# Attention of the sample group: score and value matmuls cut into four column groups of 32

## The chip, the cores and the metric

The kernel runs on one core of a Trainium2 chip. The metric is the device time of one execution in microseconds (us), as the median of several executions.

## The reference

One inference step of a two-layer decoder trunk over two groups of tokens with shared weights: a prompt of 1024 tokens and 8 samples of 4 new tokens each (32 tokens, `NS`). Width is 1024, 16 heads of 64. Layer 0 mixes by a gated short convolution, layer 1 by stick-breaking attention; each layer then has a ConvFFN of hidden width 2816. A final norm ends it. Everything is float32.

The stage in question is the attention of the samples. Each sample has 256 past tokens in two pages of 128 and its own 4 new tokens. With `z = q.k / 8 + bias_h`, over the keys s before the query t:

```
log_keep = where(mask, log_sigmoid(-z), 0)
after    = cumsum(log_keep, reverse) - log_keep
w        = where(mask, exp(log_sigmoid(z) + after), 0)
o        = einsum('bhqk,bkhd->bqhd', w, v)
```

The keys and values of the past are read through a page table that is known only at run time.

## The kernel before, in words

Each engine has a program of its own, written out in order; semaphores tie them. Weights are streamed tile by tile by SP (SyncE) as `raw`, split by GpSimd into a high and a low half (`w_hi`, `w_lo`), and TensorE does three fp32r matmuls per tile and block (lines 442, 445, 446). That is how all projections and FFNs run. The prompt attention follows the QKV projection (lines 555 to 615); after it comes the sample attention, and then the output projection `wo` and the second FFN.

The sample attention works on pairs of samples, `bp` = 0 to 3. A pair fills 128 rows: row 64*b + 4*head + t for sample b of the pair. `q_rows` holds the queries with zeros, so that chunk c of the features (heads 2c and 2c+1) has nonzero columns only at the rows of these two heads. Each chunk's matmul thus adds to the rows of its heads, and eight chunks make all heads.

- `sample_scores(bp)` (line 669) on TensorE: for each of 8 chunks and each of 2 samples one matmul with 64 columns of weights and 256 keys as the moving side (line 678); the two samples write partitions 0 to 63 and 64 to 127. Then 8 matmuls with all 128 columns against the 32 new keys (line 683), and one that adds the mask (line 685).
- ScalarE takes two sigmoids of the scores (`beta_s`, `keep_s`; line 997 onwards). VectorE scans and multiplies (`sample_weigh`, lines 1326 and 1328).
- `sample_turn(bp)` (line 688): three transposes of the weights by TensorE; VectorE copies them to `w_ts` (`sample_copy`, lines 1332 and 1333).
- `sample_values(bp)` (line 696): w times v. Two matmuls with 32 rows and 128 columns against the new values (`v_new`, line 704), then 8 matmuls with 64 columns against the V pages (line 712), each 512 wide: all heads of a half of the features. The result is 128 x 1024, over two PSUM banks. All rows get all 16 heads' features, and only the diagonal blocks (a row's own head) are used.
- `sample_rows(bp)` (line 1003) on ScalarE copies these 128 x 1024 to `o_rows`; `sample_out(bp)` (line 717) turns them in 8 transposes (line 722) into both banks of `spare`; `sample_take(bp)` (line 1335) on VectorE picks the diagonal blocks in 16 copies of 64x8 (line 1344) into `mixed`.

TensorE's order is: scores of pair 0; then for each pair `bp`: scores of bp+1, `sample_out` of bp-1, turn of bp, values of bp; at the end `sample_out` of the last pair. ScalarE has one code line for all its activations (line 744).

The pages come on SP's queue. Four page buffers of K and four of V hold two pairs. Pages of pairs 0 and 1 are loaded long before. For pairs 2 and 3 SP goes in this order: four K loads of 512 KB for pair 2 (line 393), after scores of pair 0; four V loads for pair 2 (line 399), after values of pair 0; the page numbers for pair 3, read with register loads (line 385); four K loads for pair 3, after scores of pair 1; four V loads for pair 3, after values of pair 1. SP's wait for a pair's values thus also stands ahead of the next pair's K loads. At the same time ScalarE's queue brings back x (8 times 528 KB), which was spilled to memory.

An fp32 matmul is two instructions with the same line in the trace, each with a load of weights of its own (LDWEIGHTS, engine PEld); a transpose is one.

Of the kernel before, what the change touches and what calls it, by code (L numbers as in the profile page):

```python
# [21 lines left out]
P = 128  # L22
D = 1024
KC = D // P
SEQ = 1024
NB, NT = 8, 4
NS = NB * NT
# [7 lines left out]
PAGES, PG = 2, 128  # L35
PAST = PAGES * PG
# [109 lines left out]
def build(nc, x_in, weights, taps_sc, taps_ffn, state_sc, state_ffn, gains, bias_heads, bias_rows,  # L146
# [6 lines left out]
    with ctx:  # L153
# [7 lines left out]
        def at(offset, name, shape, dt):  # L161
            return nc.alloc_sbuf_tensor_at(name, shape, dt, offset=offset)

        def size(shape, dt):
            n = 1
            for d in shape[1:]:
                n *= d
            return -(-n * (2 if dt == bf16 else 4) // 32) * 32

        def sb(name, shape, dt=f32):  # L170
            t = at(top[0], name, shape, dt)
            top[0] += size(shape, dt)
            assert top[0] <= base + arena, name
            return t
# [10 lines left out]
        ident = sb("ident", [P, P])  # L185
# [18 lines left out]
        mixed = sb("mixed", [P, KC, T])  # L204
# [15 lines left out]
        k_s = sb("k_s", [P, KC, NS])  # L220
# [16 lines left out]
        page_k = [sb(f"page_k{n}", [P, KC, PAGES, PG]) for n in range(4)]  # L237
        page_v = [sb(f"page_v{n}", [P, PAGES, D]) for n in range(4)]
# [2 lines left out]

        q_rows = [sb(f"q_rows{n}", [P, KC * (P + 2 * NT)]) for n in range(2)]
        v_new = sb("v_new", [NS, D])
        o_rows = sb("o_rows", [P, D])
        beta_s = [sb(f"beta_s{n}", [P, PAST + NS]) for n in range(2)]
        keep_s = [sb(f"keep_s{n}", [P, PAST + NS]) for n in range(2)]
        prod_s = sb("prod_s", [P, PAST + NS])
        w_ts = sb("w_ts", [P, PAGES + 1, P])
# [4 lines left out]
        out = [bank[0], bank[1]]  # L253
        spare = bank[2]
# [4 lines left out]
        score = [out[1][:, 0:2, :].rearrange("p a b -> p (a b)"), spare[:, :, :].rearrange("p a b -> p (a b)")]  # L259
# [2 lines left out]

        turned = [out[0][:, 2, :], out[1][:, 2, :]]
        attended = out[0][:, 1, :]
        o_s = out[0][:, 0:2, :].rearrange("p a b -> p (a b)")

        def sem(name):
            return ctx.enter_context(nc.semaphore(name))
# [12 lines left out]
        s_o_rows = sem("s_o_rows")  # L281
        s_o_turned = sem("s_o_turned")
# [56 lines left out]
        s_out = sem("s_out")  # L339
# [99 lines left out]
        def _(pe):  # L439
# [225 lines left out]
            for c in range(KC):  # L665
                mm = nc.tensor.transpose(score[1][0:NS, c * P:(c + 1) * P], v_s[:, c, :], ident[:, :])
            mm.then_inc(s_vturned, 1)

            def sample_scores(bp):

                pe.wait_ge(s_set, bp + 1)
                bank_s = out[1][:, bp % 2, :]
                for b in range(2):
                    pe.wait_ge(page_k_in[2 * (bp % 2) + b], (bp // 2 + 1) * 32)
                for c in range(KC):
                    for b in range(2):
                        slot, rows = 2 * (bp % 2) + b, slice(64 * b, 64 * b + 64)
                        nc.tensor.matmul(bank_s[rows, 0:PAST], q_rows[bp % 2][:, c * P + 64 * b:c * P + 64 * b + 64],  # L678
                                         page_k[slot][:, c, :, :].rearrange("p g t -> p (g t)"),
                                         start=c == 0, stop=c == KC - 1, skip_group_check=True)  # L680

                for c in range(KC):
                    nc.tensor.matmul(bank_s[:, PAST:PAST + NS], q_rows[bp % 2][:, c * P:(c + 1) * P], k_s[:, c, :],
                                     start=c == 0, stop=False, skip_group_check=True)
                nc.tensor.matmul(bank_s[:, PAST:PAST + NS], ident_b[:, :], new_b[:, bp, :], start=False,
                                 stop=True, skip_group_check=True).then_inc(s_scored, 1)

# [8 lines left out]
            def sample_values(bp):  # L696

                pe.wait_ge(s_wt, bp + 1)

                if bp:  # L700
                    pe.wait_ge(s_o_rows, bp)

                for half in range(2):
                    nc.tensor.matmul(out[0][:, half, :], w_ts[0:NS, PAGES, :], v_new[:, 512 * half:512 * half + 512],
                                     start=True, stop=False, skip_group_check=True)
                for b in range(2):
                    pe.wait_ge(page_v_in[2 * (bp % 2) + b], (bp // 2 + 1) * 32)
                for half in range(2):
                    for g in range(PAGES):
                        for b in range(2):  # L710
                            slot, rows = 2 * (bp % 2) + b, slice(64 * b, 64 * b + 64)
                            mm = nc.tensor.matmul(out[0][rows, half, :], w_ts[:, g, rows],
                                                  page_v[slot][:, g, 512 * half:512 * half + 512], start=False,
                                                  stop=g == PAGES - 1, skip_group_check=True)
                mm.then_inc(s_full, 1)

            def sample_out(bp):
                pe.wait_ge(s_o_rows, bp + 1)

                pe.wait_ge(s_out, bp + 1)  # L720
                for c in range(KC):
                    mm = nc.tensor.transpose(score[1][:, c * P:(c + 1) * P], o_rows[:, c * P:(c + 1) * P], ident[:, :])
                mm.then_inc(s_o_turned, 1)

            sample_scores(0)
            pe.wait_ge(s_vnew, 1)
            for bp in range(NB // 2):
                if bp + 1 < NB // 2:
                    sample_scores(bp + 1)
                if bp:  # L730
                    sample_out(bp - 1)
                sample_turn(bp)
                sample_values(bp)
            sample_out(NB // 2 - 1)
            pe.wait_ge(s_out, NB // 2 + 1)
            tiles_of("wo", T_WO, H_WO)
# [5 lines left out]
        def _(act):  # L742
            def act_op(o, i, func=ACT.Copy, **kw):
                return nc.scalar.activation(o, i, func, **kw)  # L744
# [257 lines left out]

            def sample_rows(bp):
                act.wait_ge(s_full, bp + 3)
                act_op(o_rows[:, :], o_s).then_inc(s_o_rows, 1)

            sample_sigmoids(0)
            for bp in range(NB // 2):
                if bp + 1 < NB // 2:
                    sample_sigmoids(bp + 1)  # L1010
                sample_rows(bp)
# [19 lines left out]
        def _(dve):  # L1031
            V = nc.vector
# [302 lines left out]
            def sample_take(bp):  # L1335

                dve.wait_ge(s_o_turned, bp + 1)
                for h in range(2):
                    rows = slice(DH * h, DH * h + DH)
                    o = mixed[rows, :, SEQ + bp * 2 * NT:SEQ + (bp + 1) * 2 * NT].rearrange("p c (b t) -> p c b t", b=2)  # L1340

                    r = score[1][rows, :].rearrange("p (c b r) -> p c b r", c=KC, b=2)
                    for c in range(KC):
                        last = V.tensor_copy(o[:, c, :, :], r[:, c, :, 8 * c + 4 * h:8 * c + 4 * h + NT])
                last.then_inc(s_out, 1)

            sample_q(0)
# [4 lines left out]
            for bp in range(NB // 2):  # L1352
                sample_copy(bp)
                if bp + 2 < NB // 2:
                    sample_q(bp + 2)
                if bp + 1 < NB // 2:
                    sample_weigh(bp + 1)
                if bp:
                    sample_take(bp - 1)
            sample_take(NB // 2 - 1)  # L1360

            for n in range(2):
# [113 lines left out]
```

## Time and profile before

| | us |
|---|---|
| median of 3 runs | 2736.73 (2732.05 to 2737.2) |
| profiled execution, its own time | 2740.34 |
| its span, first to last instruction | 2738.3 |
| TensorE matmuls busy | 2612.5 (95%) |
| VectorE busy | 1450.5 (53%) |
| ScalarE busy | 508.7 (19%) |
| GpSimd busy | 715.5 (26%) |
| DMA | 149.00 MB, mean 54 GB/s |

Busy time of TensorE counts modelled ends of matmuls that overlap, so a stream of matmuls is better read by its starts. "PEclk" is the granted clock of TensorE: 1.00 is 2.4 GHz and 0.50 is 1.2 GHz. A DMA share of 1.0 means that all 16 engines of the core are busy. In the rows PE is TensorE's matmuls, PEld its weight loads, DVE VectorE, ACT ScalarE, POOL GpSimd and SPq the queue of SP.

### The profile page before, as it was taken

To read this page: it belongs to the slowest core of one execution; us is meant where nothing else is said; L and a number is where in the kernel's file an instruction comes from. 1 tells how busy PE (TensorE), PEld (TensorE's weight loads), DVE (VectorE), ACT (ScalarE), POOL (GpSimd) and SP (SyncE) were. 2 spreads that over 40 slices of the span, in tenths; PEclk is the share of its full clock that TensorE was granted. 3 is DMA by queue.
4 is the path that set the end of the run, shared out by engine and by line. 5 is a ranking of instruction groups with operands and counts; after the bars stand their busy time and mean duration, and the time that the engine had idled before them with its cause. 6 is when DMAs were issued, how large, how long until landed. Compare 5 with 4: busy or idle time off the path is not lost.

```text
span 2738.3 us, 40374 instructions
## 1 busy us (share of the span) xinstructions
PE 2612.5 (95%) x16774; PEld 2474.4 (90%) x16774; DVE 1450.5 (53%) x1328; ACT 508.7 (19%) x905; POOL 715.5 (26%) x405
## 2 busy tenths in 40 slices
PE   6999999999999999988999999789999999999995
PEld 6999999999999999977888888559899999999995
DVE  6333436444444444466777777633654444444446
ACT  3000112000000000124444444420200000000012
POOL 3333323322233332321111111002323222333332
PEclk9999999999999999999999999999999999999997
DMA  3111111111111111131111111631111111111111
GB/s 128 47 47 47 41 46 46 41 46 47 47 47 47 40 46 39 50 110 39 40 40 40 40 47 40 206 120 47 39 39 47 47 47 47 47 47 47 47 42 63
DMA packets 58213, 149.00 MB, mean 54 GB/s; under 512 B 5458, under 2 KB 25682, under 8 KB 58066
## 3 DMA queue, kind: packets, MB, share of 16 engines
q1 hardware_dynamic: 49186, 122.42, 13.8%
q10 hardware_dynamic: 8880, 24.29, 2.3%
q8 instruction: 132, 2.16, 0.3%
q14 instruction: 15, 0.12, 0.0%
HBM read 128.91 MB, written 17.78 MB: 54 GB/s over the span
## 4 chain that ended last, share of the span: by engine, by line
PE 88%; DVE 7%; issue 2%; ACT 2%; DMA 1%; SPq 0%; DVEq 0%; ACTq 0%
PE bank L442 26%; PE bank L446 26%; PE bank L445 25%; PE bank L615 3%; PE bank L555 3%; PE bank L588 2%; DVE h_lo L1062 1%; DVE x L1160 1%; DVE y L1150 1%; ACT a_hi L744 1%; DVE total L1072 1%; DVE h_lo L1108 1%; PE bank L453 1%; PE bank L558 0%; PE bank L678 0%
## 5 line engine op out<-in xcount | busy, mean ns | idle before, releaser
L442 PE MATMUL bank<-h_hi,w_hi 128*128 128x352 f32 x3648 | 1195.5, 328 | 40.2 <-DVE h_lo L1062 21.7
L446 PE MATMUL bank<-h_hi,w_lo 128*128 128x352 f32 x3648 | 1179.4, 323 | 0.0
L445 PE MATMUL bank<-h_lo,w_hi 128*128 128x352 f32 x3648 | 1175.5, 322 | 0.0
L442 PEld LDWEIGHTS bank<-h_hi,w_hi 128*128 128x128 f32 x3648 | 688.1, 189 | 56.6 <-issue 36.6
L416 POOL CAST w_hi<-raw 128x1024 fp32r<-128x1024 f32 x196 | 212.5, 1084 | 1960.9 <-PE bank L442 1914.1
L445 PEld LDWEIGHTS bank<-h_lo,w_hi 128*128 128x128 f32 x3648 | 692.7, 190 | 0.0
L446 PEld LDWEIGHTS bank<-h_hi,w_lo 128*128 128x128 f32 x3648 | 688.7, 189 | 0.0
L418 POOL TENSOR_TENSOR w_lo<-raw,w_hi 128x1024 fp32r<-128x1024 f32 x196 | 493.2, 2517 | 15.7
L1160 DVE TENSOR_TENSOR x<-x,bank 128x1056 f32<-128x1056 f32 x192 | 238.8, 1251 | 319.1 <-PE bank L446 319.1
L442 PE MATMUL bank<-a_hi,w_hi 128*128 128x352 f32 x1056 | 343.4, 325 | 8.5 <-DVE x L1160 8.5
L445 PE MATMUL bank<-a_lo,w_hi 128*128 128x352 f32 x1056 | 341.5, 323 | 0.0
L446 PE MATMUL bank<-a_hi,w_lo 128*128 128x352 f32 x1056 | 340.8, 323 | 0.0
L1139 DVE TENSOR_TENSOR ext<-bank,rstd 128x1056 f32<-128x1056 f32 x44 | 55.4, 1259 | 344.2 <-PE bank L446 344.1
L442 PEld LDWEIGHTS bank<-a_hi,w_hi 128*128 128x128 f32 x1056 | 198.3, 188 | 16.8 <-DVE x L1160 16.3
L1263 DVE TENSOR_TENSOR_SCAN prod<-keep 128x895 f32<-128x895 f32 (+7 forms) x128 | 195.0, 1524 | 15.6 <-ACT keep L744 11.3
L445 PEld LDWEIGHTS bank<-a_lo,w_hi 128*128 128x128 f32 x1056 | 198.3, 188 | 0.0
L446 PEld LDWEIGHTS bank<-a_hi,w_lo 128*128 128x128 f32 x1056 | 198.3, 188 | 0.0
L744 ACT ACTIVATE smp<-ext 128x32 f32<-128x32 f32 x52 | 12.0, 231 | 965.4 <-DVE ext L1139 878.7
L744 ACT ACTIVATE beta<-bank,bias_pair 128x896 f32<-128x896 f32 (+7 forms) x128 | 95.0, 742 | 221.3 <-PE bank L558 217.3
L1152 DVE TENSOR_TENSOR a_lo<-y,a_hi 128x1056 fp32r<-128x1056 f32 x44 | 106.8, 2428 | 52.4 <-ACT a_hi L744 52.4
L1267 DVE TENSOR_TENSOR beta<-beta,prod 128x895 f32<-128x895 f32 (+7 forms) x128 | 127.2, 994 | 4.4
L1114 DVE TENSOR_SCALAR y<-ext,tap_ffn 128x1024 f32<-128x1024 f32 x44 | 115.8, 2631 | 9.7 <-DVE ext L1139 9.6
(104 smaller groups left out, 1654.3 us busy)
## 6 DMA issues: line engine op xcount, KB each, us to landing
raw<-weights SPq DMA_DIRECT2D x196, 512.0 KB, 3.4
page_k<-cache_k SPq DMA_DIRECT2D x16, 512.0 KB, 7.0
page_v<-cache_v SPq DMA_DIRECT2D x16, 512.0 KB, 6.3
x_spill<-x ACTq DMA_DIRECT2D x8, 528.0 KB, 6.4
k_out<-k_t ACTq DMA_DIRECT2D x8, 528.0 KB, 2.7
v_out<-v_t ACTq DMA_DIRECT2D x8, 528.0 KB, 2.7
x<-x_spill ACTq DMA_DIRECT2D x8, 528.0 KB, 7.4
y_out<-y_rows ACTq DMA_DIRECT2D x3, 1408.0 KB, 5.2
```

What stands on the lines that cost most here:

```text
L416: nc.gpsimd.tensor_copy(w_hi[ring][:, :], raw[slot][:, :]).then_inc(w_high, 1)
L418: nc.gpsimd.tensor_tensor(w_lo[ring][:, :], raw[slot][:, :], w_hi[ring][:, :].bitcast(f32), ALU.subtract).then_inc(w_split, 1)
L442: mm = nc.tensor.matmul(o, w_hi[w][:, c0:c0 + P], hi, start=first, stop=False)
L445: nc.tensor.matmul(o, w_hi[w][:, c0:c0 + P], lo, start=False, stop=False)
L446: return nc.tensor.matmul(o, w_lo[w][:, c0:c0 + P], hi, start=False, stop=last)
L555: nc.tensor.matmul(score[h][:, n0:n1], q_t[par][rows, i * P:(i + 1) * P], k_t[par][rows, n0:n1], start=True, stop=n1 < width)
L744: return nc.scalar.activation(o, i, func, **kw)
L1114: V.tensor_scalar(o[:, 0:SEQ], e[:, 0:SEQ], tap(0), None, ALU.mult).then_inc(tapped, 1)
L1152: V.tensor_tensor(a_lo[:, slot, par, :], y[par][:, :], a_hi[:, slot, par, :].bitcast(f32), ALU.subtract).then_inc(a_ready, 1)
L1160: V.tensor_tensor(xx, xx, result(s), ALU.add).then_inc(taken[s], 1)
L1263: V.tensor_tensor_scan(prod[:, width - 1:0:-1], back, back, 1.0, ALU.mult, ALU.bypass).then_inc(scanned, 1)
L1267: V.tensor_tensor(w[:, 0:width - 1], w[:, 0:width - 1], prod[:, 1:width], ALU.mult).then_inc(weighed, 1)
```

## The change

Row 64*b + 32*g + ... holds heads 0 to 7 of sample b for g = 0 and heads 8 to 15 for g = 1. The change gives each of these four groups of 32 rows matmuls of its own, with 32 columns of weights. Chunks 0 to 3 concern only the groups g = 0 and chunks 4 to 7 only g = 1, so the number of score matmuls on pages stays at 16 for a pair, in the order b, g inside each of four rounds. The 8 matmuls against the new keys become 16. The values of a group need only the 512 features of its 8 heads: the result is 128 x 512 in one bank, the two matmuls on `v_new` with 128 columns become 4 with 32, and the 8 on V pages with 64 columns become 8 with 32. The bank alternates with the pair. The row copy is 128 x 512 into one of two `o_rows`, the transposes are 4 into one of two banks of `spare`, and the take is 8 copies of 64x16. Waits are for the use two pairs ago where they were for the last one.

```diff
-        o_rows = sb("o_rows", [P, D])
+        o_rows = [sb(f"o_rows{n}", [P, D // 2]) for n in range(2)]
...
-        o_s = out[0][:, 0:2, :].rearrange("p a b -> p (a b)")
+        o_s = [out[0][:, n, :] for n in range(2)]
+        o_turned = [spare[:, n, :] for n in range(2)]
...
-                for c in range(KC):
+                for cc in range(KC // 2):
                     for b in range(2):
-                        slot, rows = 2 * (bp % 2) + b, slice(64 * b, 64 * b + 64)
-                        nc.tensor.matmul(bank_s[rows, 0:PAST], q_rows[bp % 2][:, c * P + 64 * b:c * P + 64 * b + 64],
-                                         page_k[slot][:, c, :, :].rearrange("p g t -> p (g t)"),
-                                         start=c == 0, stop=c == KC - 1, skip_group_check=True)
-
-                for c in range(KC):
-                    nc.tensor.matmul(bank_s[:, PAST:PAST + NS], q_rows[bp % 2][:, c * P:(c + 1) * P], k_s[:, c, :],
-                                     start=c == 0, stop=False, skip_group_check=True)
+                        for g in range(2):
+                            c, r = cc + g * KC // 2, 64 * b + 32 * g
+                            nc.tensor.matmul(bank_s[r:r + 32, 0:PAST], q_rows[bp % 2][:, c * P + r:c * P + r + 32],
+                                             page_k[2 * (bp % 2) + b][:, c, :, :].rearrange("p g t -> p (g t)"),
+                                             start=cc == 0, stop=cc == KC // 2 - 1, skip_group_check=True)
+
+                for cc in range(KC // 2):
+                    for b in range(2):
+                        for g in range(2):
+                            c, r = cc + g * KC // 2, 64 * b + 32 * g
+                            nc.tensor.matmul(bank_s[r:r + 32, PAST:PAST + NS], q_rows[bp % 2][:, c * P + r:c * P + r + 32],
+                                             k_s[:, c, :], start=cc == 0, stop=False, skip_group_check=True)
...
-                if bp:
-                    pe.wait_ge(s_o_rows, bp)
-
-                for half in range(2):
-                    nc.tensor.matmul(out[0][:, half, :], w_ts[0:NS, PAGES, :], v_new[:, 512 * half:512 * half + 512],
-                                     start=True, stop=False, skip_group_check=True)
+                if bp >= 2:
+                    pe.wait_ge(s_o_rows, bp - 1)
+
+                for r in range(0, P, 32):
+                    g = r // 32 % 2
+                    nc.tensor.matmul(o_s[bp % 2][r:r + 32, :], w_ts[0:NS, PAGES, r:r + 32],
+                                     v_new[:, 512 * g:512 * g + 512], start=True, stop=False, skip_group_check=True)
                 for b in range(2):
                     pe.wait_ge(page_v_in[2 * (bp % 2) + b], (bp // 2 + 1) * 32)
-                for half in range(2):
-                    for g in range(PAGES):
-                        for b in range(2):
-                            slot, rows = 2 * (bp % 2) + b, slice(64 * b, 64 * b + 64)
-                            mm = nc.tensor.matmul(out[0][rows, half, :], w_ts[:, g, rows],
-                                                  page_v[slot][:, g, 512 * half:512 * half + 512], start=False,
-                                                  stop=g == PAGES - 1, skip_group_check=True)
+                for page in range(PAGES):
+                    for r in range(0, P, 32):
+                        b, g = r // 64, r // 32 % 2
+                        mm = nc.tensor.matmul(o_s[bp % 2][r:r + 32, :], w_ts[:, page, r:r + 32],
+                                              page_v[2 * (bp % 2) + b][:, page, 512 * g:512 * g + 512], start=False,
+                                              stop=page == PAGES - 1, skip_group_check=True)
...
-                pe.wait_ge(s_out, bp + 1)
-                for c in range(KC):
-                    mm = nc.tensor.transpose(score[1][:, c * P:(c + 1) * P], o_rows[:, c * P:(c + 1) * P], ident[:, :])
+                pe.wait_ge(s_out, max(bp, 1))
+                for cc in range(KC // 2):
+                    mm = nc.tensor.transpose(o_turned[bp % 2][:, cc * P:(cc + 1) * P],
+                                             o_rows[bp % 2][:, cc * P:(cc + 1) * P], ident[:, :])
...
-                act_op(o_rows[:, :], o_s).then_inc(s_o_rows, 1)
+                if bp >= 2:
+                    act.wait_ge(s_o_turned, bp - 1)
+                act_op(o_rows[bp % 2][:, :], o_s[bp % 2]).then_inc(s_o_rows, 1)
...
-                    r = score[1][rows, :].rearrange("p (c b r) -> p c b r", c=KC, b=2)
-                    for c in range(KC):
-                        last = V.tensor_copy(o[:, c, :, :], r[:, c, :, 8 * c + 4 * h:8 * c + 4 * h + NT])
+                    r = o_turned[bp % 2][rows, :].rearrange("p (c b g r) -> p c b g r", c=KC // 2, b=2, g=2)
+                    for c in range(KC // 2):
+                        last = V.tensor_copy(o[:, c, :, :, :], r[:, c, :, :, 8 * c + 4 * h:8 * c + 4 * h + NT])
```

## Rows read from the trace of the kernel before

**Rows 1.** The page, part 1: busy us, share of the span, instructions.
```profile
PE 2612.5 (95%) x16774; PEld 2474.4 (90%) x16774; DVE 1450.5 (53%) x1328; ACT 508.7 (19%) x905; POOL 715.5 (26%) x405
```

**Rows 2.** Windows, stage: start:end, us, busy by engine, PEclk, DMA share, GB/s.
```profile
1767.95:1829.90 61.95, 52.80 (x320) 29.14 (x320) 14.74 (x87) 7.69 (x13) 0.00 (x0) 0.95 0.59 196
```

**Rows 3.** Windows of 2 us, for the granted clock (third number from the end).
```profile
1770.00:1772.00 2.00, 2.00 (x16) 1.18 (x14) 0.00 (x0) 0.00 (x0) 0.00 (x0) 0.77 0.99 395
1812.00:1814.00 2.00, 2.00 (x7) 0.60 (x8) 0.58 (x8) 0.00 (x0) 0.00 (x0) 0.50 0.00 0
1834.00:1836.00 2.00, 2.00 (x9) 2.00 (x9) 2.00 (x2) 2.00 (x3) 1.92 (x2) 0.56 0.00 0
```

**Rows 4.** Chain of waits through the stage: start us, us, what.
```profile
1767.95 5.12 PE bank L678 x32
...
1787.19 0.35 SPq L399
...
1791.83 0.56 SPq L393
...
1795.62 6.85 DMA page_k<-cache_k
...
1802.61 3.67 PE bank L678 x32
...
1812.24 5.14 PE bank L712 x16
...
1829.10 0.76 DVE mixed L1344 x8
```

**Rows 5.** Who waited for whom, 1760 to 1835: total us, times, longest.
```profile
PE bank L678 <- DMA page_k<-cache_k: 2.6, 1, 2.6
```

**Rows 6.** Timeline of TensorE streams: start us, us, engine, line, tiles, count.
```profile
1782.12 0.18 PEld L704 LDWEIGHTS bank<-v_new,w_ts 32*128 32x128 f32 x1 [0.24 <-issue]
1782.55 0.18 PEld L704 LDWEIGHTS bank<-v_new,w_ts 32*128 32x128 f32 x1 [0.24 <-issue]
1784.41 0.14 PEld L712 LDWEIGHTS bank<-page_v,w_ts 128*64 128x64 f32 x2 [0.29 <-issue]
1784.84 0.14 PEld L712 LDWEIGHTS bank<-page_v,w_ts 128*64 128x64 f32 x2 [0.28 <-issue]
1783.50 3.65 PE L712 MATMUL bank<-page_v,w_ts 128*64 128x512 f32 x16
1774.92 3.67 PE L678 MATMUL bank<-page_k,q_rows 128*64 128x256 f32 x32
1773.00 1.97 PE L683 MATMUL bank<-k_s,q_rows 128*128 128x32 f32 x16
1759.01 0.88 PE L615 MATMUL bank<-w_first,v_rows 128*64 128x128 f32 x12 [1.70 <-ACT w_first L744]
1827.29 1.09 PE L722 MATMUL bank<-ident,o_rows 128*128 128x128 f32 x8 [1.12 <-ACT o_rows L744]
```

**Rows 7.** Timeline of ScalarE and VectorE: row copies, weights of pair 0, the take.
```profile
1826.21 1.02 ACT L744 ACTIVATE o_rows<-bank 128x1024 f32<-128x1024 f32 x1 [7.79 <-PE bank L712]
1776.81 0.46 DVE L1328 TENSOR_TENSOR beta_s<-beta_s,prod_s 128x287 f32<-128x287 f32 x1
1765.11 0.60 ACT L744 ACTIVATE mixed<-bank 128x512 f32<-128x512 f32 x1 [0.79 <-PE bank L615]
1828.42 1.43 DVE L1344 COPY mixed<-bank 64x8 f32<-64x8 f32 x16 [6.53 <-PE bank L722]
1767.51 0.39 DVE L1316 COPY q_rows<-q_s 64x64 f32<-64x64 f32 x2
```

**Rows 8.** Windows of 0.5 us, for the DMA engines (last two numbers).
```profile
1784.50:1785.00 0.50, 0.50 (x6) 0.20 (x4) 0.00 (x0) 0.00 (x0) 0.00 (x0) 1.00 0.24 71
1786.00:1786.50 0.50, 0.50 (x4) 0.14 (x2) 0.00 (x0) 0.00 (x0) 0.00 (x0) 1.00 0.00 0
1788.50:1789.00 0.50, 0.50 (x8) 0.35 (x6) 0.00 (x0) 0.00 (x0) 0.00 (x0) 1.00 0.65 229
```

More of the change, by code:

```diff
@@ L1339, in sample_take @@
                     rows = slice(DH * h, DH * h + DH)
-                    o = mixed[rows, :, SEQ + bp * 2 * NT:SEQ + (bp + 1) * 2 * NT].rearrange("p c (b t) -> p c b t", b=2)
-                    r = score[1][rows, :].rearrange("p (c b r) -> p c b r", c=KC, b=2)
-                    for c in range(KC):
-                        last = V.tensor_copy(o[:, c, :, :], r[:, c, :, 8 * c + 4 * h:8 * c + 4 * h + NT])
+                    o = mixed[rows, :, SEQ + bp * 2 * NT:SEQ + (bp + 1) * 2 * NT].rearrange("p (g c) (b t) -> p c b g t", g=2, b=2)
+                    r = o_turned[bp % 2][rows, :].rearrange("p (c b g r) -> p c b g r", c=KC // 2, b=2, g=2)
+                    for c in range(KC // 2):
+                        last = V.tensor_copy(o[:, c, :, :, :], r[:, c, :, :, 8 * c + 4 * h:8 * c + 4 * h + NT])
                 last.then_inc(s_out, 1)
```

## The prediction

> **What bounds the kernel now.** I read the page first [rows 1]: TensorE is busy for 95% of the span, so time taken off its stream is time off the end, unless a transfer is late there. The diff touches one stage only. The chain of waits puts it between the first score matmul at 1767.95 us and the last copy of the sample outputs, which ends at 1829.88 [rows 4]: 61.95 us, 2.3% of the span, with TensorE busy for 52.80 us and the DMA engines at 0.59 [rows 2]. That is all the change can touch.
>
> Read in order, the chain [rows 4] says what ends last inside it. Up to 1787.2 it is TensorE. Then it leaves TensorE: the end of the first values lets SP issue the V pages of pair 2 (1787.19), behind them SP reads page numbers and issues the K pages of pair 3 (1791.83), and the chain waits for these until 1802.6. TensorE had done its work by 1800.1 and stood 2.6 us for them [rows 5]. From 1802.61 to 1829.88 (27.3 us) nothing is loaded that anybody waits for, and the path is TensorE with one ScalarE copy and one set of VectorE copies per pair. So the stage has three parts: TensorE, page transfers, TensorE again.
>
> **Does four in turn overlap as two do?** Each fp32 matmul is two instructions in the trace. With all 128 columns of weights the 512-wide one starts every 0.43 us, one at a time (1782.12, 1782.55); with 64 columns two start together every 0.43 us [rows 6]. So two column groups overlap completely: 16 instructions are 8 steps of 0.43 (3.65 us with the tail of the last), and the 32 score instructions at 256 wide are 16 steps of 0.216 (3.67 us) [rows 6]. The number of instructions stays: 32 for scores, 16 for page values. Only if four groups overlap are there 8 and 4 steps. Nothing in this trace has four groups at once; the bounds are a step of four at the price of a step of two (all saved) and at the price of four single ones (each step twice as long for the same count). I take the first, because the second member of a pair adds nothing that can be seen (0.43 against 0.43), and the groups write different partitions.
>
> The Trainium skill (TensorE: Matmul & The Clock Gate, section Measured speedup vs the span model) gives 2.38 for three column tiles with 512 columns, not 3. By that a step of four would be a quarter longer, 0.27 and 0.54 by estimate, and the tail below would lose 1.8 us of its gain. This trace has full overlap at two and none of three.
>
> **Working, from 1802.6 to the end** (warm clock):
> - Scores of pair 3: 8 steps of 0.216 fewer: -1.73.
> - Scores against the new keys: now 16 instructions, 0.112 apart, 1.97 us [rows 6]. They become 32 with a quarter of the weights and 32 columns. Bounds: 0.22 us, if four groups overlap and time scales with columns from 0.216 for 256; and 1.74, if an instruction can't be fed faster than the fastest stream here, 12 in five steps of 0.11 plus the tail (0.88 us), 0.054 each [rows 6]. I take 0.9, between them: -0.9 (ends 0 and -1.6).
> - v_new: 4 single steps of 0.43 become 8 instructions in 2 steps, in values of pairs 2 and 3: 2 x -0.86 = -1.72.
> - Page values: 8 steps become 4: 2 x -1.72 = -3.44.
> - Transposes of the outputs: 8 become 4, at 0.109 each (1.09 us for 8 [rows 6]); three calls lie on the path: 3 x -0.44 = -1.31.
> - ScalarE's copy of the rows: 128x1024 took 1.02, and a 128x512 out of PSUM 0.60 [rows 7]: 2 x -0.42 = -0.84. It is exposed for pairs 2 and 3 and hidden behind scores for 0 and 1.
> - The last take: 16 copies of 64x8 in 1.43 us, 0.09 each; 8 copies of 64x16 at about 0.1 (64x64 costs 0.2) [rows 7]: -0.65. The takes before it lie beside page values.
> - The transpose, copy and wait from the weights to v_new (1.2 to 1.3 us, twice) stay.
>
> Sum -10.6. The new waits (the row copy on the turning of two pairs ago, the turning on the take of two pairs ago) are looser than those replaced, and nothing queues behind them.
>
> The Trainium skill (TensorEngine Tiling, section Instruction Overhead) speaks against splitting the new-key matmuls: some 60 cycles each, so a short free dimension should not be tiled. By that estimate 32 take 0.8 us and not 0.2, and the sum stays within 0.1 of the above. No row here has such short ones in column groups.
>
> **The clock.** TensorE's granted clock was 0.5 (1.2 GHz) when the stage began and full from about 1771 (0.77 in that window); it fell to 0.5 again at 1812 [rows 3], and the page values of pair 2 took 5.14 [rows 4] instead of 3.65 [rows 6]: +1.5 in the time before. After the change TensorE stands longer for pages (about 5 us twice, below), and its work between the waits of the tail is half as long. The bounds: no low stretch (-1.5), or low for the whole tail, whose TensorE streams then sum to 9.8 us (scores 1.73 and 0.9, turnings of outputs 3 x 0.44, of weights 2 x 0.35, v_new 2 x 0.86, pages 2 x 1.72), so +9.8 - 1.5. The next stage too began at 0.5, until shortly before 1836 (0.56 in the window before [rows 3]), some 3.3 us of matmuls, which costs 1.7. I take one such stretch and a little, 2.2 in place of 1.5: +0.7. Tail: -9.9.
>
> **Before 1802.6.** Score streams of pairs 0 and 1 save 1.9 (partly cold) and 1.75, the new keys about 0.9 each, the values of pair 0 0.86 + 1.72: they end 8 us earlier, at about 1779. The chain from the scores of pair 0 to its weights ends at 1777.27 with VectorE's multiplication (1776.81 and 0.46 [rows 7]), 2.3 us after these scores, and so still fits beside the scores of pair 1. But the pages don't come 8 us earlier. From 1766.5 to 1784 the DMA engines are full (0.99 in the first window of rows 3) with x coming back (8 times 528 KB) and the K pages of pair 2; the last bytes of these land at about 1786, and the engines idle only until the V pages start at about 1788.4 [rows 8]. Order in the one queue stays: K2, V2, K3. V2 is now issued before K2 is in, so V2 starts between 1784.5 (engines thinning to 0.24) and 1786: 2.4 to 3.9 us earlier. K3 follows as before, since its issues are ready in time (4.6 us after V2's). I take -3.3. So of 8 us some 5 turn into TensorE standing for K2 and then for K3. The other transfers: V3 is issued after K3 and lands 5 to 7 us after it, before values of pair 3 need it; weights for the next stage are already split three tiles ahead.
>
> Sum -3.3 - 9.9 = **-13.2 us**. The profiled execution took 2740.34 for its span of 2738.3; the runs' median 2736.73 is 3.6 lower, a fixed offset that I keep: 2736.73 - 13.2 = **2723.5 us**.
>
> **Rivals.**
> - A, four overlap, as above: 2723.5. Its own range: saving 7.6 (K3 2.4 earlier, new keys nothing, clock +4.5, half way to D) to 17 (3.9, new keys -1.6, no low clock): 2720 to 2729. Chance 0.74.
> - B, the change doesn't do what it says: only two at a time are in flight, for example because the two halves of one matmul share a group and a step takes the late half of one and the early half of the next. For it: the pairs in rows 6 can be read so. Against it: the first step has two already, and the count of steps is exactly half that of instructions. Scores, v_new and page values stay; the new keys -0.9, transposes -1.3, copies -0.84 and -0.65 in the tail, and V2 issued about 1.8 us earlier by two new-key streams: -4.2 (2.8 to 5.5), 2732.5. Chance 0.12.
> - C, slower: 32-column matmuls run one after another, in the score and value streams. Scores +3.46, page values +3.44, v_new +1.72 per pair. On the path before K3 stand two score streams and one of values (+12), in the tail one and two (+13.8), less 2.8: +23, 2760. For it: four moving streams from memory at once are nowhere in the trace. Against: two don't disturb each other. Between B and C the cost is linear: it turns slower once more than about 0.15 of the overlap of pairs is lost. Chance 0.05.
> - D, four overlap but the clock is low for the whole tail: -10.6 + 8.3 - 3.3 = -5.6, 2731. For it: the drop at 1812 came with TensorE partly idle. Against: 5 us of busy time at 1766 raised it. Chance 0.07. 0.02 is left for others.
>
> A measurement of this kernel can tell about 0.2% (5.5 us) from no change. A and half of D are faster, B and the rest the same, C slower: 0.79, 0.15, 0.06. The range takes A from below and B and D from above: 2718 to 2733.5.
>
> **What would show it.** Four 32-column instructions starting within some 20 ns, every 0.216 us in scores and 0.43 in values; scores of 1.9 us and page values of 1.9. Two waits of TensorE for page_k, of 4 to 7 us each, where there was one of 2.6. DMA engines without a hole at 1786 to 1788. Less than 18 us from the scores of pair 3 to the last take. I am wrong if starts come in twos (B) or singly (C), if K3 lands as long after the stage's start as before, or if the granted clock is 0.5 for more than 5 us after K3.

## The result, and the profile after

Five executions of the changed kernel: median 2715.28 us (2712.78 to 2722.12), against 2736.59 (2732.05 to 2737.2) for five of the kernel before; ratio 0.9932, 95% interval 0.9918 to 0.9946. That is 21.3 us less, below the forecast's range. Twelve more executions, taken with the experiments, gave medians of 2720.54 and 2719.87 for six each. All 17 together have a median of 2719.87 and a mean of 2719.2; all 95 executions of the kernel before 2736.57 and 2736.4. So the change is worth 17.2 us (15.3 to 19.1, from the means), 0.6% of the kernel. A part of the first 21.3 was the luck of five executions: their median lies 4.7 us below that of the next twelve (2720.0).

The chain of waits of the changed kernel through the stage (start us, us, what); compare [rows 4]:

```profile
1759.50 3.33 PE bank L680 x32
...
1765.09 4.42 SPq L394
1769.70 2.47 SPq L394
1772.27 1.61 SPq L400
...
1778.18 0.56 SPq L394
...
1782.98 6.84 DMA page_k<-cache_k
...
1789.95 3.46 PE bank L680 x32
...
1796.40 1.90 PE bank L717 x16
...
1805.40 0.46 DVE mixed L1352 x4
```

The stage begins at 1759.50 and ends at 1805.86: 46.4 us instead of 61.9. TensorE leaves the chain after the first scores; from 1763 to 1790 the chain is SP's issuing and the page transfers. K of pair 3 is there 30.5 us after the start, not 34.7; from there to the end it is 15.9 us, not 27.3.

The timeline of the changed kernel, for [rows 6] and [rows 7] (start us, us, engine, line, tiles, count):

```profile
1768.29 0.13 PEld L717 LDWEIGHTS bank<-page_v,w_ts 128*32 128x32 f32 x4 [0.30 <-issue]
1768.72 0.13 PEld L717 LDWEIGHTS bank<-page_v,w_ts 128*32 128x32 f32 x4 [0.30 <-issue]
...
1789.95 3.46 PE L680 MATMUL bank<-page_k,q_rows 128*32 128x256 f32 x32 [2.96 <-DMA page_k<-cache_k]
...
1793.22 0.48 PE L688 MATMUL bank<-k_s,q_rows 128*32 128x32 f32 x32
...
1795.34 1.06 PE L710 MATMUL bank<-v_new,w_ts 32*32 32x512 f32 x8 [0.70 <-DVE w_ts L1341]
...
1796.33 1.92 PE L717 MATMUL bank<-page_v,w_ts 128*32 128x512 f32 x16
...
1798.32 0.60 ACT L750 ACTIVATE o_rows<-bank 128x512 f32<-128x512 f32 x1 [3.56 <-PE bank L717]
...
1804.29 0.66 PE L727 MATMUL bank<-ident,o_rows 128*128 128x128 f32 x4 [0.72 <-ACT o_rows L750]
1804.98 0.87 DVE L1352 COPY mixed<-bank 64x16 f32<-64x16 f32 x8 [3.59 <-PE bank L727]
```

Four loads start together every 0.43 us where two did, and in the trace the four matmuls of a step start within 20 ns (at 1796.33 the first four, the next four 0.45 us later): 16 page-value instructions take 1.92 us instead of 3.65. The 32 short ones against the new keys take 0.48 where 16 took 1.97.

Waits for pages, and windows (as in [rows 2], [rows 3] and [rows 8]) of the changed kernel:

```profile
PE bank L680 <- DMA page_k<-cache_k: 11.2, 2, 8.2
```

```profile
1759.50:1805.85 46.35, 29.96 (x384) 13.49 (x384) 12.53 (x55) 5.96 (x12) 0.00 (x0) 0.82 0.80 262
1776.00:1778.00 2.00, 0.02 (x3) 0.05 (x4) 0.00 (x0) 0.00 (x0) 0.00 (x0) 0.50 1.05 384
1790.00:1792.00 2.00, 2.00 (x20) 1.05 (x24) 0.00 (x0) 0.00 (x0) 0.00 (x0) 0.50 1.04 414
1796.00:1798.00 2.00, 2.00 (x20) 0.42 (x16) 1.21 (x9) 0.00 (x0) 0.00 (x0) 1.00 0.00 0
60.00:360.00 300.00, 295.55 (x1857) 294.73 (x1856) 105.41 (x88) 24.72 (x48) 96.98 (x52) 1.00 0.14 45
```

Two waits, 8.2 and 3.0 us, where there was one of 2.6; the DMA share of the stage rose from 0.59 to 0.80. Behind each wait the granted clock is 0.50, and the scores pay for it: those of pair 2 take 3.64 us and those of pair 3 3.46, not 1.93.

The last row is of a stretch that nobody touched. The same window of the kernel before:

```profile
60.00:360.00 300.00, 295.54 (x1833) 294.72 (x1833) 103.70 (x88) 23.58 (x47) 93.56 (x50) 1.00 0.14 45
```

In the same 300 us, at full clock and equally busy, TensorE did 1833 matmuls there and 1857 here. Inside the stream (pauses of over 200 ns left out) the mean distance of two starts is 160.9 and 158.9 ns. By 1280 us the changed kernel's profile was 10.5 us ahead, all in code that the change does not touch, and its stage began at 1759.5 instead of 1768.0. So the two profiled executions, 25.1 us apart, differ by 15.6 in the stage, by 8.5 ahead of it and by 1.1 behind it.

### The profile page after: what moved, and what is told of

The parts are those of the page before. It is cut to its first block, busy times and chain, and to the rows that moved or that the text cites. A ratio compares the mean times of both kernels' runs of the same rounds, so it can differ in the third digit from the quotient of the medians.

```text
span 2713.2 us, 40471 instructions
## 1 busy us (share of the span) xinstructions
PE 2580.6 (95%) x16838; PEld 2451.0 (90%) x16838; DVE 1447.0 (53%) x1296; ACT 507.6 (19%) x905; POOL 715.4 (26%) x405
## 4 chain that ended last, share of the span: by engine, by line
PE 87%; DVE 7%; issue 3%; ACT 2%; SPq 1%; DMA 1%; DVEq 0%; ACTq 0%
PE bank L443 27%; PE bank L447 26%; PE bank L446 26%; PE bank L616 3%; PE bank L556 3%; PE bank L589 2%; DVE h_lo L1070 1%; DVE x L1168 1%; DVE y L1158 1%; ACT a_hi L750 1%; DVE total L1080 1%; PE bank L454 1%; PE bank L559 0%; SPq L394 0%; DVE y_rows L1386 0%
## 5 line engine op out<-in xcount | busy, mean ns | idle before, releaser
L419 POOL TENSOR_TENSOR w_lo<-raw,w_hi 128x1024 fp32r<-128x1024 f32 x196 | 493.3, 2517 | 15.7
L1122 DVE TENSOR_SCALAR y<-ext,tap_ffn 128x1024 f32<-128x1024 f32 x44 | 114.9, 2612 | 10.5 <-DVE ext L1147 10.4
```

The lines of the kernel that those rows point to most:

```text
L419: nc.gpsimd.tensor_tensor(w_lo[ring][:, :], raw[slot][:, :], w_hi[ring][:, :].bitcast(f32), ALU.subtract).then_inc(w_split, 1)
L1122: V.tensor_scalar(o[:, 0:SEQ], e[:, 0:SEQ], tap(0), None, ALU.mult).then_inc(tapped, 1)
```

## The experiments

All kernels ran beside executions of the kernel before on the same chip. "Start" and "stage" are from the trace of one execution (first score matmul on a page; from there to the last take's end), "K3" is the start of the scores of pair 3 after the stage's start.

| kernel | median us (executions) | ratio to before, 95% | start | K3 | stage |
|---|---|---|---|---|---|
| before | 2736.59 (5) | | 1768.0 | 34.7 | 61.9 |
| e1, before again | 2736.12 (12) | 0.9984 to 1.0006 | 1762.9 | 34.4 | 63.4 |
| changed | 2715.28 (5) | 0.9918 to 0.9946 | 1759.5 | 30.5 | 46.4 |
| e2, changed again | 2720.54 (6) | 0.9923 to 0.9958 | 1767.5 | 30.7 | 46.7 |
| e16, changed, third | 2719.87 (6) | 0.9921 to 0.9950 | 1764.7 | 31.6 | 50.2 |
| e3, scores only | 2730.47 (12) | 0.9971 to 0.9993 | 1759.7 | 30.2 | 55.9 |
| e4, values only | 2725.79 (8) | 0.9945 to 0.9976 | 1767.1 | 31.6 | 53.6 |
| e5, group by group | 2724.01 (4) | 0.9945 to 0.9974 | 1758.5 | 31.9 | 50.3 |
| e6, new keys whole | 2722.62 (5) | 0.9926 to 0.9964 | 1767.6 | 33.5 | 49.4 |
| e7, x later | 2716.38 (6) | 0.9926 to 0.9950 | 1764.0 | 27.1 | 43.1 |
| e8, x later, numbers first | 2716.99 (6) | 0.9920 to 0.9945 | 1761.4 | 27.4 | 43.4 |
| e9, before, x later | 2736.40 (11) | 0.9993 to 1.0011 | 1757.6 | 37.9 | 66.8 |
| e10, K straight | 2715.70 (6) | 0.9905 to 0.9940 | 1762.7 | 27.4 | 43.4 |
| e11, K straight, x later | 2719.00 (6) | 0.9917 to 0.9953 | 1767.0 | 25.0 | 43.5 |
| e12, before, K straight | 2732.58 (10) | 0.9969 to 0.9999 | 1764.5 | 32.9 | 58.5 |
| e13, waits filled | 2719.33 (6) | 0.9922 to 0.9954 | 1767.3 | 30.9 | 46.7 |
| e14, K straight, filled | 2712.55 (6) | 0.9899 to 0.9931 | 1760.6 | 27.4 | 41.8 |
| e15, K straight, x later, numbers | 2712.76 (5) | 0.9892 to 0.9927 | 1764.4 | 22.8 | 38.7 |
| e17, e15 and waits filled | 2708.87 (4) | 0.9881 to 0.9914 | 1764.4 | 24.1 | 38.5 |

**The same kernels again (e1, e2, e16)**, without an edit.

> The kernel before, unchanged, once more with a profile of its own. The profile after shows the stage of the sample attention 15.6 us shorter (61.9 to 46.4), while the medians differ by 21.3; the rest is in code that the change does not touch, most of it ahead of the stage (the stage starts at 1759.5 instead of 1768.0). Theory R (the speed of the untouched matmul streams differs from one execution to the next, by some 0.4%): the stage takes 61.5 to 62.5 us again, its start lies anywhere between 1757 and 1768, and the median is within 0.2% of before. Theory S (the change also moves something that makes the untouched code quicker, every time): the stage starts at 1766 to 1769 again, and the mean step of the fp32r stream between 60 and 260 us is 161 ns as in the profile before.

> The changed kernel, unchanged, once more. Theory R: the stage takes 46 to 48 us, its start lies anywhere between 1757 and 1768, the median anywhere from 2713 to 2723. Theory S: the start is 1757 to 1761 again, the mean step of the early fp32r stream is 158.9 ns, and the median is 2712 to 2717.

> The changed kernel once more. Stage 46 to 48 us, start anywhere in 1757 to 1768, median 2715 to 2723; with the eleven executions so far it should be 15.5 to 18 below the kernel before.

Theory R holds. The kernel before started its stage at 1762.9 with a mean distance of 158.9 ns, the changed one at 1767.5 with 161.0: the quick stream belongs to an execution and not to a kernel. (e1's stage, 63.4, is 0.9 longer than R allowed: the page values of both pair 2 and pair 3 ran at the low clock, 5.30 and 5.12 us.) Over all traces the start lies between 1757.6 and 1768.0, without order. e16's stage is 50.2 and not 46 to 48, which I had not expected: TensorE was at 0.5 for the scores of pair 3 and again for the values of pair 3.

**The halves apart (e3, e4).** e3 takes `sample_scores` of the changed kernel and all else of the kernel before; e4 the opposite.

> Only the scores (pages and new keys) in four groups of 32; values, row copies, transposes and take as before. Theory of the stage (the K and V pages of pairs 2 and 3 form a chain in the one queue that the scores and values of pairs 0 and 1 only start earlier): the work ahead of the first V load is 6 to 7 us shorter, the K pages of pair 3 come only 3 to 4.5 us earlier after the start of the stage, and the part after them is 1.5 to 3 us shorter; the stage takes 55 to 57.5 us, the median is 5 to 7 lower than before. Rival (pages are no limit, every saved TensorE us counts): stage 12 to 13 us shorter.

> Only values, row copy, transposes and take in the new form; scores as before. Theory of the stage: the V load of pair 2 is issued 2.6 us earlier and lands the K pages of pair 3 about 2.4 earlier, and the part after these is 8 us shorter, 9.5 if TensorE's clock stays up; stage 50 to 52 us. With e3 the sum of the savings is 14 to 17, near the 15.6 of both. Rival (pages no limit): 4 x 2.6 for values and 4 x 0.4 for transposes and 2 us of tail, 14 us alone.

e3 is as the page theory has it: 55.9, with K3 at 30.2 (4.4 earlier), and far from the 12 to 13 us of its rival. In e4 K3 comes 3.0 earlier, near the 2.4; its stage is 1.6 over the expectation, and its scores and values of pair 3 ran at the low clock (6.40 us against 3.67 in the kernel before, and 3.29 against 1.92 in the changed one). Against 62.6, the mean of the two traces of before, e3 saves 6.7 and e4 9.0: 15.7 for both. The medians, against those of the kernel before beside them, say 6.3 and 11.0, together 17.3.

**The order of the groups (e5).** The loops over chunk and page go inside those over the group:

```
-                for cc in range(KC // 2):
-                    for b in range(2):
-                        for g in range(2):
+                for b in range(2):
+                    for g in range(2):
+                        for cc in range(KC // 2):
...
-                for page in range(PAGES):
-                    for r in range(0, P, 32):
+                for r in range(0, P, 32):
+                    for page in range(PAGES):
```

> The changed kernel with another order only: in the scores on pages and the values on pages all matmuls of one group of 32 columns come one behind the other, then the next group's. Same instructions, same results. Theory (four overlap only because neighbours in the program are of different groups): 32 score instructions take about 6.9 us instead of 1.7 warm, 16 value instructions 6.9 instead of 1.9; the K pages of pair 3 come near 41 us after the stage's start instead of 30.5, the stage takes 68 to 74 us, the kernel 2740 to 2748. Rival (TensorE takes matmuls of other groups from further back in its queue): stage 46 to 50 us, no difference.

The theory fell. Timeline of e5, TensorE, pairs 1 (scores, L680 and L688) and 0 (values, L717):

```profile
1765.31 3.95 PE L680 MATMUL bank<-page_k,q_rows 128*32 128x256 f32 x29
1768.88 0.26 PE L688 MATMUL bank<-k_s,q_rows 128*32 128x32 f32 x6
1769.10 0.60 PE L680 MATMUL bank<-page_k,q_rows 128*32 128x256 f32 x2
1769.32 0.26 PE L688 MATMUL bank<-k_s,q_rows 128*32 128x32 f32 x6
1769.53 0.38 PE L680 MATMUL bank<-page_k,q_rows 128*32 128x256 f32 x1
...
1772.35 1.94 PE L717 MATMUL bank<-page_v,w_ts 128*32 128x512 f32 x16
```

With four instructions per group in a row the values overlap as fully as before (1.94 us). With eight per group the 32 page scores take 4.6 us (1765.31 to 1769.91), neither 1.9 nor 6.9. And twelve matmuls against new keys, which stand behind all page scores in the program, start ahead of the last of these; all four calls of the trace show it. By these starts TensorE takes work of another group from further back in its queue; how far back, no run measures. So "four in turn" is worth 2.7 us per pair in the scores here and nothing in the values. The rival was right for the values and not for the scores: the stage is 50.3 us, against 46.4 to 50.2 with the clock in between, and the median 4.1 above that of the 17.

**New keys whole (e6)**, as before the change, 8 matmuls with 128 columns:

```
+                for c in range(KC):
+                    nc.tensor.matmul(bank_s[:, PAST:PAST + NS], q_rows[bp % 2][:, c * P:(c + 1) * P], k_s[:, c, :],
+                                     start=c == 0, stop=False, skip_group_check=True)
```

> The changed kernel with the scores against the new keys as before: 8 matmuls with 128 columns instead of 16 with 32. Theory (32 short instructions in four groups take 0.4 us where 16 whole ones took 1.8; of the four calls only pair 3's lies behind the pages): the part from the scores of pair 3 on is 1.4 to 1.9 us longer, stage 47.5 to 48.5 us against 46.4 and 46.7. Rival (short instructions are bound by issue, as the prediction's 0.9 had it): the call takes within 0.5 us of the split one.

Chain of e6: values of pair 1, then the scores of pair 3.

```profile
1797.70 3.57 PE bank L714 x16
1801.27 1.74 PE bank L680 x32
1803.01 1.90 PE bank L685 x16
```

1.90 where the split call takes 0.3 in the chain (0.48 with its tail): the call is 1.5 to 1.6 longer, as the theory has it, and the rival falls. The whole part from the scores of pair 3 on was not longer (15.7 us, against 15.9 and 16.0), since the scores ran at full clock here; against e14's, which has no low stretch (14.4), it is 1.3 longer. The stage is 0.9 over the expectation: the values of pair 1 ran at the low clock (3.57), and TensorE came to the scores of pair 3 only at 33.5, when the pages were there already.

**What the pages wait for (e7 to e12, e15).** x later moves x's eight loads on ScalarE's queue behind the row copy of pair 2; numbers first reads all page numbers at the head of SP's trip; K straight changes the tile, and with it the K loads and the scores' reading, which are not shown:

```
-            for f in range(KC):
-                act.dma_start(x[:, f, :], x_spill[f, :, :]).then_inc(x_back, 16)
...
                 sample_rows(bp)
+                if bp == 2:
+                    for f in range(KC):
+                        act.dma_start(x[:, f, :], x_spill[f, :, :]).then_inc(x_back, 16)
...
-                    ids = [page(n, g) for n in (2 * pair, 2 * pair + 1) for g in range(PAGES)]
+                all_ids = [page(n, g) for n in range(4) for g in range(PAGES)]
...
-        page_k = [sb(f"page_k{n}", [P, KC, PAGES, PG]) for n in range(4)]
+        page_k = [sb(f"page_k{n}", [P, PAGES, KC, PG]) for n in range(4)]
```

> The changed kernel with x brought back (8 times 528 KB on ScalarE's queue) after the row copy of pair 2 instead of ahead of the stage. Theory (after the change the stage waits for pages, and these share the DMA engines with x): the K pages of pair 2 are there 13 to 14 us after the stage's start instead of 18.5, those of pair 3 at 24 to 26 instead of 30.5, the stage takes 39.5 to 41.5 us instead of 46.4, the median falls by 5 to 7 below the changed kernel's. Rival (the page chain is held by SP's issuing and by its own latencies, not by x): stage within 1.5 us of 46.4.

> As the last one, and SP reads all eight page numbers of a trip before its first wait, so nothing stands between the V loads of pair 2 and the K loads of pair 3. If the transfers are now the limit, the K pages of pair 3 come at 24 to 26 us as without it (0 to 1 us earlier); if SP's 2.9 us of number reads are the limit, 2 to 3 us earlier, stage 37 to 38.5 us.

> The kernel before with x brought back after the row copy of pair 2. Theory (before the change x cost the pages nothing, since K of pair 2 was in before TensorE wanted it and x had landed long before V of pair 2): the K pages of pair 3 again 34 to 35 us after the stage's start, stage 61.5 to 63.5 us, the median within 0.15% of before. Rival (x always cost): stage 3 us or more shorter.

> The changed kernel with the tile of a K page laid out as in memory (page, chunk, key instead of chunk, page, key), so each partition's 4 KB come in one piece instead of eight of 512 bytes; the scores read it with a stride. Theory (the stage waits for the DMA engines, and K pages move at 290 GB/s where V pages and x move at 410): K pages of pair 2 come 16 to 17 us after the stage's start instead of 18.4, those of pair 3 at 26 to 28 instead of 30.5, stage 42.5 to 44.5 us. Rival (the page chain is bound by latencies between loads): stage within 1 us of 46.5.

> Both: K pages in one piece, and x brought back after the row copy of pair 2. Theory: K of pair 2 at 11.5 to 13 us, K of pair 3 at 22 to 24.5, so TensorE hardly waits; stage 37.5 to 40 us, median 6 to 9 below the changed kernel's. Rival (with x gone the transfers no longer bind and only one of the two helps): stage 42 to 43.5 as with x later alone.

> The kernel before with the K pages in one piece. Theory: its one wait for pages, at the scores of pair 3, was 2.6 us long, and the load of these pages gets 2 us shorter: stage 59.5 to 61 us where the clock falls as in the profile before (61.9), and up to 3 us more for each further low stretch. Rival (the strided reading makes the scores slower): scores of a pair over 3.8 us.

> K pages in one piece, x later, page numbers read first. Theory (with both transfers shortened, K of pair 3 waited for its issue behind SP's 2.9 us of number reads): K of pair 3 at 22 to 23.5 us instead of 25.0. Rival (V of pair 2 ahead of it in the queue is what it waits for): 24.5 to 25.

The direction is right for K3 in e7, e10, e11 and e15, and the size mostly too large. x later brings K of pair 2 from 18.4 to 14.6 and K3 from 30.5 to 27.1, not 24 to 26: behind K of pair 2, V and the next K need another 12.5 us by themselves. Its stage of 43.1 missed the 39.5 to 41.5, and its median is 3.5 below that of the 17, which the intervals can't tell from nothing. Number reads cost nothing as long as the transfers bind (e8 like e7). With K straight K3 is at 27.4 and the stage at 43.4, as expected. With both K3 is at 25.0, just outside the 22 to 24.5; the stage missed the 37.5 to 40 and at 43.5 has the rival's number for another reason, since scores and values of pair 3 ran at the low clock. Then the reads do hold K3: e15 has it at 22.8. These are single traces, and e17, whose page loads are those of e15, has K3 at 24.1, so differences of about 1 us between them are not shown. In the kernel before none of this was binding: e9's median is unchanged, as expected. Its K3 of 37.9 and its stage of 66.8 are not, and the chain of e9 shows why (values of pair 0, scores of pair 3, values of pair 3):

```profile
1771.73 3.77 PE bank L704 x4
1775.50 5.16 PE bank L712 x16
...
1795.49 5.36 PE bank L678 x32
...
1815.51 5.31 PE bank L712 x16
```

Three low stretches, against about 2.0, 3.6, 3.7 and 3.6 warm [rows 4, 6]. e12 had none in its tail, and its stage was 58.5, 1 us below the expectation; strided reading cost its scores nothing:

```profile
1797.47 3.67 PE bank L678 x32
```

**The clock apart (e13, e14, e17).** Matmuls that nobody reads stand ahead of the scores of pairs 2 and 3 (32 and 12 in e13, 27 and 8 in e14, 7 and 16 in e17):

```
+                for n in range({2: 32, 3: 12}.get(bp, 0)):
+                    nc.tensor.matmul(out[0][:, 2, 0:P], mean[:, :], ident[:, :], start=True, stop=True)
```

> The changed kernel, and ahead of the scores of pair 2 and pair 3, where TensorE waits 8.2 and 3.0 us for K pages, 32 and 12 fp32 matmuls of 128 columns and 128 wide (0.21 us each warm, 6.9 and 2.6 us) into a piece of PSUM that nobody reads; the output is not touched. Theory (the waits cost the pages' lateness and, on top, the low clock after them: scores of pair 3 took 3.27 instead of 1.7 us): clock full for the scores of pairs 2 and 3, pages at the same times (18.4 and 30.5), stage 44.5 to 45.5 us instead of 46.4. Rival (low stretches come from the gaps of the part behind the pages): scores of pair 3 warm, but a low stretch in values of pair 2 or 3 instead, stage 46 to 48.

> K pages in one piece, and 27 and 8 such matmuls in the two waits (6.9 and 2.0 us in that kernel). Theory: pages at 17.2 and 27.4 as there, no low stretch in the values of pair 3 (3.20 us there, 1.9 warm), stage 41 to 42 us instead of 43.4. Rival: the low stretch comes back behind the pages, stage 43 to 44.5.

> K pages in one piece, x later, page numbers first, and 7 and 16 matmuls that nobody reads (1.5 and 3.4 us) ahead of the scores of pairs 2 and 3. Theory: pages at 12.1 and 22.8 as there, scores of pair 3 at full clock (1.9 us instead of 3.2), stage 37 to 38 us instead of 38.7, median 2709 to 2713. Rival (a low stretch comes behind the pages instead): stage 38.5 to 40.

Page scores in the timelines of e13 (pairs 2 and 3), e14 (pair 3) and e15 (pairs 2 and 3):

```profile
1785.62 1.94 PE L682 MATMUL bank<-page_k,q_rows 128*32 128x256 f32 x32 [0.66 <-DMA page_k<-cache_k]
...
1798.14 3.35 PE L682 MATMUL bank<-page_k,q_rows 128*32 128x256 f32 x32 [2.87 <-DMA page_k<-cache_k]
```

```profile
1788.06 1.93 PE L682 MATMUL bank<-page_k,q_rows 128*32 128x256 f32 x32 [1.95 <-DMA page_k<-cache_k]
```

```profile
1776.56 1.93 PE L681 MATMUL bank<-page_k,q_rows 128*32 128x256 f32 x32 [1.88 <-DMA page_k<-cache_k]
...
1787.23 3.17 PE L681 MATMUL bank<-page_k,q_rows 128*32 128x256 f32 x32 [3.90 <-DMA page_k<-cache_k]
```

In e13 the filled wait of pair 2 leaves the scores warm, 1.94 us and not 3.64; but the next pages come when they come, and nothing is gained. Ahead of pair 3 2.87 us stayed unfilled and the scores were slow: stage unchanged at 46.7, the theory's 44.5 to 45.5 missed, and the slow scores are not the rival's pattern either. In e14 the tail had no low stretch and the stage was 41.8, as expected and 1.6 shorter than e10's; but the tails of e2 and e7 have no low values either, with nothing filled, so that the filling did it is not shown. In e17 the scores of pair 3 took 1.92 us in the chain and not 3.13, but its pages came 1.3 later than in e15, so its stage of 38.5 is only 0.2 shorter, just outside the 37 to 38. e17 is the quickest version found, 1.0% below the kernel before; its interval and those of e14 and e15 overlap.

## Why the prediction was wrong

The mechanism was right and the size was not: 13.2 us forecast, 21.3 in the first five executions, 17.2 (15.3 to 19.1) in all. Term by term, from the chains:

- **Four overlap**: right, completely. A step of four costs 0.43 and a step of two cost 0.43. The Trainium skill (TensorE: Matmul & The Clock Gate, section Measured speedup vs the span model) has 2.38 for three column tiles; this trace does not agree, four instructions take the time of one.
- **Scores of pair 3, -1.73**: right at full clock (1.93 against 3.67).
- **New keys, -0.9**: too small, 1.97 to 0.48 is -1.5. I had taken a middle between 0.22 and 1.74 for the call; the truth lies near the lower end, since the groups overlap here too. The 0.8 us estimated from the Trainium skill (TensorEngine Tiling (Array Packing), section Instruction Overhead) is 0.3 more than the trace has.
- **v_new, values, transposes, row copy, take**: -1.72, -3.44, -1.31, -0.84, -0.65 forecast; -1.84, -3.42, -1.31, -0.84, -0.56 measured. In the warm tails (e12, 25.6 from K3 to the end, against e14, 14.4) all terms with the new keys make -11.2; forecast -10.6.
- **Clock, +0.7**: not there. Above those warm tails the kernel before lost 1.7 and 3.3 in its two traces and the changed one 1.5, 1.6 and 4.2: means of 2.5 and 2.4. The longer waits do bring the low clock, but the low matmuls are half as long.
- **Pages, -3.3**: near. K3 moved from 34.5 (mean of two traces) to 30.9 (of three): -3.6. That the hole in the DMA engines closes and TensorE then waits twice was right; the waits were 8.2 and 3.0 us, not 5 and 5. The prediction's own figures (values done at 1779, K of pair 2 in at 1786) would have made the first one 7.
- **Sum in the stage**: the means of these traces are 62.6 and 47.8, -14.9 against the -13.2 forecast.

**The step that failed** is the range, and below it two terms of the sum. Its low end, 2718, lies 2 us below A's own 2720, a saving of 17 added up from the terms of the stage alone; nothing stands in it for how far executions of one and the same kernel lie apart. "A fixed offset that I keep" shows the same gap: the base of 2736.73 was sound (95 executions give 2736.57), but the 3.6 us between the profiled execution and the median were no property of the kernel, and in the changed kernel's first profile they are 0. The stage starts anywhere from 1757.6 to 1768.0, though nothing ahead of it is touched, and the 95 executions lie between 2728.6 and 2747.4. The terms that were mis-sized are the clock (+0.7, measured -0.1) and the new keys (-0.9, measured -1.5).

Of the 8.1 us between 13.2 and 21.3, the terms are thus 1.7, and 4.1 are the luck of the first five executions (21.3 against 17.2). The other 2.3, between the stage's -14.9 and the -17.2 of the executions, stay open. The traces have the changed kernel 1.5 us quicker ahead of the stage and 1.7 behind it (907.3, 908.0 and 908.2 us to the end of the program against 908.4 and 910.7), which two and three traces can't tell from nothing. Better terms alone would not have saved the range: they give 2721.8, still 6.5 above the first median. The median of the 17, 2719.87, lies inside it.

B, C and D are excluded: starts come in fours, and the clock was low for a part of the tail only.

## What to carry to other kernels

Where fp32 matmuls have few useful columns of weights, cutting them into four column groups paid by the full factor here, short ones included; put neighbours in different groups when one group has more than a few in a row. After such a cut read the chain again: here two thirds of what TensorE saved ahead of the last pages became waiting for transfers (the waits grew by 8.6 us, from 2.6 to 11.2, and K3 came 4.2 earlier), and a straight layout of the pages, page numbers read first and another time for x together brought the stage from 46.4 to 38.7 and the median 7.1 below that of the 17. Before setting a range, look at how far executions of the same kernel lie apart, and let that in, whatever the terms say.

## What the runs showed of the hardware that I had not expected

- By the trace, TensorE starts matmuls out of program order across column groups: in e5 six of a later line went ahead of two of an earlier one. The Trainium skill (TensorE: Matmul & The Clock Gate, section The mechanism) says that matmuls start strictly in order; this trace disagrees.
- The same fp32r stream at full clock has a mean distance of 158.9 ns in one execution and 160.9 in the next, for hundreds of us.
- A page load with pieces of 4 KB and the same bytes came sooner than one with 512 bytes: K3 at 27.4 instead of 30.5 with nothing else changed.
- SP was held in its issues of K pages: 6.9 us for two of them (from 1765.09 in the chain above), where one at 1778.18 took 0.56. It goes with the small pieces, and not only with other loads being pending. The four K issues of pair 2 take 8.72 us in the changed kernel and 4.80 with x later (e7); with x where it was and pieces of 4 KB (e10) they take 2.05. So pieces of 512 bytes cost SP's time too, and V of pair 2 is issued 12.8 us after the stage's start in the changed kernel and 10.4 in e10. The first issues of the changed kernel and of e10:

```profile
1763.44 8.72 SPq L394 DMA_DIRECT2D page_k<-cache_k  x4
```

```profile
1766.67 2.05 SPq L394 DMA_DIRECT2D page_k<-cache_k  x4
```
